# Gated DeltaNet stage: the chunk inverse's lower levels on packed 32x32 squares instead of full 128x128 matrices

## The reference, cut to what matters

```python
g = jnp.cumsum(chunks(g[..., None])[..., 0], axis=-1)
decay = jnp.where(incl, jnp.exp(jnp.where(incl, diff, 0.0)), 0.0)
kb = k * beta[..., None]
lower = jnp.where(strict, jnp.einsum("nbhid,nbhjd->nbhij", kb, k) * decay, 0.0)
t_inv = lax.linalg.triangular_solve(lower + eye, jnp.broadcast_to(eye, lower.shape),
                                    left_side=True, lower=True, unit_diagonal=True)
u = t_inv @ (v * beta[..., None])
w = t_inv @ (kb * jnp.exp(g)[..., None])
...
intra = jnp.where(incl, jnp.einsum("nbhid,nbhjd->nbhij", q, k) * decay, 0.0)

def step(s, xs):
    u_i, w_i, kd_i, gl_i, qd_i, a_i = xs
    s_next, v_new = advance(s, u_i, w_i, kd_i, gl_i)
    return s_next, qd_i @ s + a_i @ v_new
```

## Time and profile before

| | before |
|---|---|
| time, median of 3 runs | 2993.04 us (2987.51 to 2994.1) |
| time of the profiled execution | 2991.31 us |
| span of the profiled execution, first to last instruction | 2989.2 us |
| mean granted TensorE clock | 0.963 of full |
| PE busy in the span | 2713.9 us (91%) |
| DVE / ACT / POOL busy in the span | 1289.3 / 621.4 / 503.0 us |

### The profile page before, as it was taken

The page is one execution under the profiler, slowest core; times in us unless marked ns, Lnnn a source line. Parts: engine busy times, 40 slices in busy tenths (PEclk is TensorE's granted clock), DMA queues, the critical chain, the costliest instruction groups (busy, mean ns, idle before and its releaser), DMA issues. The chain is left out here.

```text
span 2989.2 us, 48287 instructions
## 1 busy us (share of the span) xinstructions
PE 2713.9 (91%) x18975; PEld 1481.9 (50%) x18975; DVE 1289.3 (43%) x1862; ACT 621.4 (21%) x1150; POOL 503.0 (17%) x514
## 2 busy tenths in 40 slices
PE   4999979999898978879999999999669999999996
PEld 3544468999543455544444444445424444333442
DVE  2566646666567066630688121113413222222231
ACT  4222233333221166640000120003100000000000
POOL 0111135555011000000000000000013332232232
PEclk7999989999999999999999999999789999999998
DMA  6111000000101000011122223112547999969622
GB/s 236 29 28 28 0 8 1 2 2 2 36 21 35 14 1 0 0 42 36 51 80 74 74 74 106 32 38 89 197 176 255 398 342 375 397 221 351 207 81 76
DMA packets 187806, 314.86 MB, mean 105 GB/s; under 512 B 13264, under 2 KB 125287, under 8 KB 187335
## 3 DMA queue, kind: packets, MB, share of 16 engines
q1 hardware_dynamic: 172519, 289.53, 26.9%
q0 software_dynamic: 15168, 23.60, 3.6%
HBM read 295.13 MB, written 22.41 MB: 106 GB/s over the span
## 5 line engine op out<-in xcount | busy, mean ns | idle before, releaser
L2399 PE MATMUL p_gate_up<-w_unit,rowsT 128*32 128x512 f32 x4672 | 521.7, 597 | 29.1 <-DVE rowsT L2455 19.2
L1786 PE MATMUL p_gate<-hT,w_gate 128*128 128x512 f32 x768 | 342.0, 598 | 7.1 <-DVE region L1910 5.8
L2399 PEld LDWEIGHTS p_gate_up<-w_unit,rowsT 128*32 128x32 f32 x4672 | 165.1, 111 | 340.9 <-issue 292.9
L1002 PE MATMUL p_w<-hT,w_c 128*128 128x512 f32 (+1 forms) x704 | 264.3, 537 | 7.5 <-ACTq L219 7.5
L2413 PE MATMUL p_y<-w_unit,hiddenT 128*32 128x256 f32 x4672 | 266.3, 379 | 1.2 <-DVE hiddenT L2465 1.2
L1786 PEld LDWEIGHTS p_gate<-hT,w_gate 128*128 128x128 f32 x768 | 144.0, 191 | 183.1 <-issue 181.4
L2451 DVE STREAM_TRANSPOSE rows_turned<-rows 128x256 f32<-128x256 f32 x74 | 33.0, 446 | 457.1 <-PE p_gate_up L2399 450.8
L2413 PEld LDWEIGHTS p_y<-w_unit,hiddenT 128*32 128x32 f32 x4672 | 165.4, 110 | 118.8 <-issue 41.4
L1002 PEld LDWEIGHTS p_w<-hT,w_c 128*128 128x128 f32 x704 | 134.9, 192 | 134.0 <-issue 121.0
L2436 ACT ACTIVATE sigmoid<-p_gate_up 128x256 f32<-128x256 f32 x73 | 28.0, 383 | 788.0 <-PE p_gate_up L2399 788.0
L1935 DVE SCALAR_TENSOR_TENSOR region<-gated,taps,region x120 | 154.1, 1284 | 16.7 <-DVE region L1935 1.3
(11 more groups left out here) (344 smaller groups left out, 3825.2 us busy)
## 6 DMA issues: line engine op xcount, KB each, us to landing
w_unit<-in_w_gate SPq DMA_DIRECT2D x128, 512.0 KB, 15.4
w_unit<-in_w_up SPq DMA_DIRECT2D x128, 512.0 KB, 16.4
w_unit<-in_w_down SPq DMA_DIRECT2D x128, 512.0 KB, 12.3
w_b<-in_w_mod SPq DMA_DIRECT2D x32, 512.0 KB, 4.8
w_gate<-in_w_in SPq DMA_DIRECT2D x24, 512.0 KB, 5.4
region<-in_w_mod SPq DMA_DIRECT2D x4, 2048.0 KB, 14.0
w_c<-in_w_in SPq DMA_DIRECT2D x16, 512.0 KB, 3.9
w_branch<-in_w_branch SPq DMA_DIRECT2D x24, 256.0 KB, 5.6
```

The costliest lines, as they stand in the source:

```text
L1002: last = nc.tensor.matmul(p_w[i % 4][:, 0:size], w[n][:, c, :], k.hT[:, c, at:at + size], start=(c == 0), stop=(c == KD - 1))
L1786: last = nc.tensor.matmul(p_g[half][:, :], wg[i][:, c, :], k.hT[:, c, CTX + at:CTX + at + 512], start=(c == 0), stop=(c == KD - 1))
L2399: last = nc.tensor.matmul(p_gu[part, :].rearrange("p (m c r) -> p m c r", m=2, r=BLK), xT[:, c, :], unit[:, :, j], start=(c == 0), stop=(c ...
```

## The change

The inverse of the levels 0 to 4 is nonzero only in the diagonal 32x32 squares. The change keeps only those. Each of the tiles `lt`, `masked`, `d`, `dt` and `x` of these levels becomes 128x128 for a direction: in partition rows 32b to 32b+31 stands square `b`, of all four heads side by side, 32 columns each. The two level masks in the constant table shrink from 7 levels of 128 columns to 5 levels of 32 columns each.

- A product of a level is 16 small products for a direction (4 heads, 4 squares; `quarters`) instead of 4 full ones (`four`). The key products are made in squares too: 4x4 of 128x32 by 128x32 for the diagonal, and the off-diagonal blocks that the two joins need by themselves (`key_halves`).
- POOL's `scale_decay` picks the four diagonal squares out of the decay tile, one instruction for each with a wait on each before the next. `scale_halves` does so for the four 32x32 and two 64x64 blocks of the joins, in tiles `lt_join32` and `lt_join64`. `assemble` copies the squares of `d` into a 64-wide tile for the second join.
- The full inverse `dt` is still needed by `solve`. It is cleared once by POOL, and filled in each step: two squares of each direction by POOL (`assemble_rest`, after `scale_halves`), two by DVE (signal `dt_far`), the rest by the joins, as before.
- DVE's `intra` moves behind `first_level`, `turn_blocks` and the new `lower_halves`. `first_level` waits for the copies of the step before, since `tp` is not doubled.
- `join32_plain` makes only the two blocks that the second join reads, not all four.

```diff
+                def scaled(dst, size, g, d, a, b):
+                    col = k.beta[size * a:size * a + size, tile(g, d), 4 * d:4 * d + 4].unsqueeze(2)
+                    return nc.gpsimd.tensor_tensor(rows_of(dst, size, a), square(at_[g % 2][d], size, a, b),
+                                                   col.to_broadcast([size, HEADS, size]), ALU.mult)
+
                 def scale_decay(g, d):
                     after(pool, "decayed", g, d)
                     after_level(pool, "masked", g - 1, TOP, d, 0, TOP)
+                    for b in QUARTERS:
+                        scaled(lp[d], 32, g, d, b, b).then_inc(s("decay_scaled"), 1)
+                        pool.wait_ge(s("decay_scaled"), 8 * g + 4 * d + b + 1)
+
+                def scale_halves(g):
                     after_both(pool, "x64", g - 1)
-                    nc.gpsimd.tensor_tensor(lt[d][:, :, :], at_[g % 2][d][:, :, :], beta(g, d), ALU.mult) \
-                        .then_inc(s("decay_scaled"), 1)
+                    for i, (d, a, b) in enumerate(HALVES[0], 1):
+                        scaled(l32, 32, g, d, a, b).then_inc(s("halves_scaled"), 1)
+                        pool.wait_ge(s("halves_scaled"), 6 * g + i)
+                    for i, (d, a, b) in enumerate(HALVES[1], 5):
+                        scaled(l64, 64, g, d, a, b).then_inc(s("halves_scaled"), 1)
+                        pool.wait_ge(s("halves_scaled"), 6 * g + i)
...
+                def assemble_rest(g):
+
+                    for b in QUARTERS:
+                        d = b // 2
+                        after(pool, "solved", g - 2, d)
+                        nc.gpsimd.tensor_copy(square(dt[g % 2][d], 32, b, b), rows_of(tp[d], 32, b)) \
+                            .then_inc(s("dt_near"), 1)
+                        pool.wait_ge(s("dt_near"), 4 * g + b + 1)
 
                 pool.wait_ge(s("table_exp"), 3)
                 for d in BOTH:
                     scale_decay(0, d)
+                scale_halves(0)
+                for i in range(2):
+                    for d in BOTH:
+                        nc.gpsimd.memset(dt[i][d][:, :, :], 0.0).then_inc(s("cleared"), 1)
+                nc.gpsimd.memset(d64[:, :, :], 0.0).then_inc(s("cleared"), 1)
+                pool.wait_ge(s("cleared"), 5)
...
+                    assemble(g)
                     if g + 1 < NCH:
                         for d in BOTH:
                             scale_decay(g + 1, d)
+                        scale_halves(g + 1)
+                    assemble_rest(g)
...
                 def key_products(g, d):
                     after_both(pe, "x32_stored" if d == 0 else "x64_stored", g - 1)
-                    four(pa[d], lambda h: kT(g, d, h), lambda h: kT(g, d, h)).then_inc(s("kk"), 1)
+                    for h in range(HEADS):
+                        for b in QUARTERS:
+                            part = kT(g, d, h)[:, 32 * b:32 * b + 32]
+                            last = nc.tensor.matmul(pa[d][32 * b:32 * b + 32, 32 * h:32 * h + 32], part, part,
+                                                    start=True, stop=True)
+                    last.then_inc(s("kk"), 1)
...
+                def quarters(bank, lhs, rhs):
+                    for h in range(HEADS):
+                        for b in QUARTERS:
+                            part = slice(32 * b, 32 * b + 32)
+                            last = nc.tensor.matmul(bank[part, 32 * h:32 * h + 32], lhs[part, h, :], rhs[part, h, :],
+                                                    start=True, stop=True)
+                    return last
...
                 def merge_part(g, n, d):
                     after_level(pe, "masked", g, n, d, 0, TOP)
                     after_level(pe, "d", g, n - 1, d, 0, TOP)
-                    four(pa[d], lambda h: lm[d][:, h, :], lambda h: dm[d][:, h, :]).then_inc(s("x"), 1)
+                    quarters(pa[d], lm[d], dp[d]).then_inc(s("x"), 1)
...
                 def first_level(g, d):
                     after_level(dve, "masked", g, 0, d, 0, TOP)
-                    after(dve, "solved", g - 2, d)
+                    if g:
+                        dve.wait_ge(s("dt_near"), 4 * g)
+                        after_both(dve, "dt_far", g - 1)
...
                     for d in BOTH:
                         lower(g, d)
-                    for d in BOTH:
-                        intra(g, d)
                     for d in BOTH:
                         first_level(g, d)
                         turn_blocks(g, 0, d)
+                    lower_halves(g)
+                    for d in BOTH:
+                        intra(g, d)
```

More of the change, by code:

```diff
@@ L93, in constant_table @@
     put("neg1", np.where(i[None, :] <= i[:, None], 0.0, -1e30))
[L94 to L98, removed]
+    j = np.arange(32)
+    for n, s in enumerate(LEVELS[:PACKED_LEVELS]):
+        m = (j[None, :] // (2 * s) == j[:, None] // (2 * s)) & (j[None, :] // s % 2 == 1) & (j[:, None] // s % 2 == 0)
+        for name, part in (("lev0", m), ("lev1", m.T)):
+            t[:, CONST[name] + 32 * n:CONST[name] + 32 * n + 32] = np.tile(part, (4, 1))
     t[:, CONST["steps"]:CONST["steps"] + 32] = BLK * np.arange(32)
@@ L1239, in after_both, with square, rows_of, bank_rows @@
                 eng.wait_ge(s(name), g + 1)
[L1241 to L1247, removed]
+        def square(t, size, row, col):
+            return t[size * row:size * row + size, :, size * col:size * col + size]
+        def rows_of(t, size, row):
+            return t[size * row:size * row + size, :, :]
+        def bank_rows(bank, size, row, at=0):
+            return bank[size * row:size * row + size, at:at + HEADS * size].rearrange("p (h n) -> p h n", h=HEADS)
+        QUARTERS = range(4)
         with nc.Block() as block:
@@ new lines, in merge, with join32_part, join32_plain @@
+                    quarters(pc[d], xp[d], tp[d]).then_inc(s("dxt"), 1)
+                def join32_part(g):
+                    for h in range(HEADS):
+                        for d, a, b in HALVES[0]:
+                            last = nc.tensor.matmul(bank_rows(pa[0], 32, b)[:, h, :], rows_of(l32, 32, a)[:, h, :],
+                                                    rows_of(dp[d], 32, a)[:, h, :], start=True, stop=True)
+                    last.then_inc(s("x32"), 1)
+                def join32_plain(g):
+                    for h in range(HEADS):
+                        for d, b in ((0, 1), (1, 2)):
+                            last = nc.tensor.matmul(bank_rows(pc[1], 32, b)[:, h, :], rows_of(tp[d], 32, b)[:, h, :],
+                                                    rows_of(x32, 32, b)[:, h, :], start=True, stop=True)
+                    last.then_inc(s("d_product"), 1)
@@ new lines, in join32, with join64_part @@
+                def join32(g):
+                    for h in range(HEADS):
+                        for d, a, b in HALVES[0]:
+                            last = nc.tensor.matmul(bank_rows(pc[0], 32, a)[:, h, :], rows_of(x32, 32, b)[:, h, :],
+                                                    rows_of(tp[d], 32, b)[:, h, :], start=True, stop=True)
+                    last.then_inc(s("dxt32"), 1)
+                def join64_part(g):
+                    for h in range(HEADS):
+                        for d, a, b in HALVES[1]:
+                            last = nc.tensor.matmul(bank_rows(pa[1], 64, b)[:, h, :], rows_of(l64, 64, a)[:, h, :],
+                                                    rows_of(d64, 64, a)[:, h, :], start=True, stop=True)
+                    last.then_inc(s("x64"), 1)
@@ L1412, in _, with join64 @@
+                def join64(g):
+                    for h in range(HEADS):
+                        for d, a, b in HALVES[1]:
+                            last = nc.tensor.matmul(bank_rows(pc[0], 64, a)[:, h, :], rows_of(x64, 64, b)[:, h, :],
+                                                    square(dt[g % 2][d], 64, b, b)[:, h, :], start=True, stop=True)
+                    last.then_inc(s("dxt64"), 1)
                 for d in BOTH:
@@ L1422, in _ @@
                     key_products(0, d)
+                key_halves(0)
                 for g in range(NCH):
```

142 lines of the change are left out of this document (86 added, 56 removed).

## The result

| | before | after |
|---|---|---|
| time, median of 20 runs each, same chip | 2989.43 us (2987.49 to 2994.28) | 2996.73 us (2990.99 to 2998.67) |
| ratio after to before | | 1.002, 95% interval 1.0013 to 1.0027 |
| span of the profiled execution | 2989.2 us | 2993.8 us |
| mean granted TensorE clock | 0.963 | 0.947 |

A forecast was written before the change was run, and what follows sets the result against it. PE was taken to set the pace, busy 35.6 of each 36.7 us step. Seven steady steps save 11 us, step 1 2, the last 2.5, together 15.5: 2978 us, range 2950 to 3035.

The forecast's parts named there:

- the level's small products and the level: DeltaNet levels: 128 records of 12 to 13 ns each; a level falls from 5.42 to 3.55 us.
- The rival built on it: Levels: small products start no faster than one in 25 ns; a step + 6 us, 3023 us; chance 0.05.
- POOL's chain: Before the values: 14 POOL instructions in a row, 5.6 us plus 1.0 of waits, about 6.6 us.
- Keys to values: From key products to values in a steady step: 5.5 us before, 10.0 after, as values wait for `intra`.
- the rival of the dear chain: POOL's 14 instructions cost more than assumed: 3016 us at 0.3 us more each, 3072 at 0.82 per wait; chance 0.22.
- the clock: After PE's gap of over 5 us in each step, the clock falls to 0.50, costing 2.1 us a step.
- clock of 1.00 in the levels: Levels, half small and half full products: PE was taken to stay at full clock there.
- the sum of the step, 35.15 us: Steady step: 9.8 + 10.0 + 2.6 + 10.65 = 33.05 us, plus 2.1 for the clock; 1.55 saved from 36.7.
- PE starves for instructions: Some 870 products a step where it had 407; four gaps, + 5 us a step, 3023 us; chance 0.08.
- Step 0: First DeltaNet step: late start from POOL instructions and clearing, given back by its four levels; 0 saved.
- Step 1: Second DeltaNet step: nothing behind levels 2 and 3; 2 us saved.
- The last step: Last DeltaNet step: loses 6 us at its start, gains 5.6 in three levels and 3 at the fourth; 2.5 saved.

The follow-up runs named there:

- the filled gap: Changed kernel plus five unread float32 products of 512 columns in TensorE's gap ahead of the values; 2972.29 us, ratio to before 0.9938.
- the early `intra`: Changed kernel with DVE's `intra` moved back ahead of `first_level`, nothing else; 2948.85 us, ratio to before 0.9863.

## Why the prediction failed, point by point

**Right: the level's small products and the level.** I had 12 to 13 ns for each record and 3.55 us for a level. The steady step's first level took 557.42 - 553.86 = 3.56 us, the next two 3.67 and 3.82, longer by the gaps inside. The rule of the Trainium skill ("TensorE: Matmul & The Clock Gate", section "Wait — 56ns, not 53.3ns?") that matmuls start no closer than some 25 ns apart does not hold for these tiles: 64 records of 32x32 begin within 0.65 us, and 166 of 128x32 within some 1.5 us, both 10 ns apart or less. The rival built on it is refuted.

**Right: POOL's chain.** The groups by shape in the stage show what no row before did:

```profile
L1276 POOL TENSOR_TENSOR masked<-lt,const 128x128 f32<-128x128 f32 x100 | 43.9, 454 | 72.9 <-PE p_a L1455 66.7 <-DVE dt L1689 4.5 <-DVE lt L1661 0.6
...
L1289 POOL TENSOR_TENSOR lt_join<-decay,beta 32x128 f32<-32x128 f32 x40 | 15.7, 392 | 3.1
L1289 POOL TENSOR_TENSOR lt_join<-decay,beta 64x256 f32<-64x256 f32 x20 | 12.2, 609 | 1.6
L1314 POOL COPY d<-d 32x128 f32<-32x128 f32 x40 | 12.1, 303 | 29.7 <-DVE d L1681 27.9
```

I had 0.40, 0.61 and 0.30 for the scalings and copies, 0.46 for the mask, and 0.07 for each wait of POOL for itself (six scalings in 3.18 us, two of 0.61 and four of 0.39, leave 0.08 for each of five waits). Keys to values: forecast 10.0, measured 9.69. The 0.82 of the earlier trace rows was no measure for it, and the rival of the dear chain is out.

**Right in mechanism, too small: the clock.** Forecast 2.1 us a step from the two falls of the earlier trace rows; measured 5.32 - 2.81 = 2.5 to 2.7 in the stretch behind the gap. The mechanism is shown by the filled gap. The section "HAM oscillation — how this bites in real kernels" of the same page of the Trainium skill told it rightly: the clock fell in each pass. The forecast's clock of 1.00 in the levels was right too, in six of the seven steady steps.

**The step that failed: the sum of the step, 35.15 us, which held nothing for PE's own instructions.** The steady steps took 260.22 / 7 = 37.17. What is missing is 2.0 us a step, 14.2 over seven, and the "issue" gaps listed in these seven steps are 11.2 us, 1.6 each, most of the miss. The rest is mainly the clock, 0.6 too small, less the chain, 0.3 too large; in the step shown these two have the same sizes, and 1.1 us are gaps, 0.5 of them listed. I had this as a rival, "PE starves for instructions", with + 5 us a step and a chance of 0.08. Its gaps happened, at a third of its size, in addition to the forecast and not in its place. I had ruled it nearly out because the one row for it stood where the memory queues were full. The queues' load was not the point, since the gaps came with the queues at 1%: the number of PE instructions in a step was, which went from 407 records to about 870 (records, not products as the prediction has it). With half the products in the levels the gaps are gone, and a steady step takes 34.1 us. What in the supply makes PE stand stays open. The saving was to be 1.55 us a step, so a third of this rival was enough to turn its sign.

**Off in the edges, 3.1 us in all.** Step 0: forecast 0, measured 34.47 - 36.78 = -2.3. Step 1: forecast -2, measured 35.11 - 36.08 = -1.0. The last step: forecast -2.5, measured +1.2. The head of the stage, not forecast: +0.65. Step 1 and the last step carry "issue" gaps and a clock below that of before (0.81 and 0.86 against 0.95 and 0.97); my sum for step 1 had no term for either. The steady steps, with a forecast of -11 and 260.22 - 256.13 = +4.1 measured, add 15.1. That makes 18.2 us between the forecast of -15.5 and the stage's +2.7.

**What followed from the order.** I named the late `intra` as what is late next, and sized it, and then treated it as given. Taken back, it is worth 48 us, three times the whole forecast. By the profile of before, with PE busy for 97% of a step, this was the line to weigh: a wait of 5 us on the engine that sets the pace, plus the clock, times eight.

## What to carry to other kernels

When an edit moves a read behind a longer chain on the engine that frees a buffer, the price is the idle time of the bound engine and its slower clock behind it; here 2.5 us of clock on top of a 5 us gap, in each step, for the order of two short loops. And when work on TensorE is cut into very short products, count instructions as well as columns: half as many products, of 64 columns in place of 32, took off 37 to 45 us with the same columns in all. Where the whole gain is a small difference of large terms, let each rival's mechanism into the sum at a part of its size, and not only as a case of its own.

## What the runs showed of the hardware that was not expected

- TensorE ran 32x32 and 128x32 float32 records at about 10 ns apiece (64 in 0.65 us of weight loads and starts, 166 in 1.64 us), and then stood for up to 2.6 us with no signal to wait for. The gaps went with the number of instructions in the stage: none listed, 19.4 and 39.2 us, with the instruction queue at about 1%.
- GpSimd's cost went little with the rows: a scaling of 32 rows by 128 columns took 392 ns, a mask of 128 rows by 128 columns 454. Its wait for its own last instruction cost 0.08 us, worked out from six scalings in 3.18 us.
- The wait of 5.2 us was followed by the lower clock for the next 5 us of full work. The wait of at most 1.4 us (the early `intra`) was not, in the step shown; but a gap of 1.72 us in the same trace was followed by 3 us at 0.50.
